# A two-layer block on one core: decay, beta and norm rows of the recurrent layer spread by DMA instead of by products

## The reference, cut to what matters

```python
proj = x @ w_in
qkv, z, b_logit, a_logit = split(proj)
qkv = silu(causal_depthwise_conv(qkv, conv_w))          # 4 taps
q = l2_normalize(q) * (Dh ** -0.5)                      # t * rsqrt(sum(t*t) + 1e-6), per head and token
k = l2_normalize(k)
beta = sigmoid(b_logit)
g = cumsum(-exp(a_log) * softplus(a_logit + dt_bias))   # per head, within a chunk
decay = exp(where(causal, g[:, None] - g[None, :], -inf))
a = (k * beta) @ k.T * decay                            # strictly lower part
m = where(strict, a, 0) + I
u, w = solve(m, [v * beta, k * beta * exp(g)])
qk = q @ k.T * decay
k_dec = k * exp(g[-1] - g)
# then: v_new = u - w @ state;  o = (q*exp(g)) @ state + qk @ v_new;  o * rms * silu(z)
```

## Time and profile before

| | us |
|---|---|
| median of three runs | 1905.39 |
| lowest, highest | 1904.49, 1906.96 |
| the profiled execution's own time (its span, first to last instruction) | 1904.5 |
| TensorE busy | 1755.1 (92%) |
| VectorE busy | 748.0 (39%) |
| ScalarE busy | 451.2 (24%) |
| chain that ended last: PE, DMA, DVE, ACT | 75%, 18%, 3%, 2% |

### The profile page before, as it was taken

One profiled execution on the slowest core, in us unless ns is written; L12 is line 12 of the kernel. 1 busy time (PEld: TensorE's weight loads), 2 busy tenths in 40 slices (PEclk: granted clock), 3 DMA queues, 4 the chain that ended last, 5 costly groups with the idle time before them and its releaser, 6 DMA issues.

```text
span 1904.5 us, 23817 instructions
## 1 busy us (share of the span) xinstructions
PE 1755.1 (92%) x9756; PEld 1111.8 (58%) x9756; DVE 748.0 (39%) x1141; ACT 451.2 (24%) x692; POOL 13.3 (1%) x20
## 2 busy tenths in 40 slices
PE   8999999999999999999999898888898888987986
PEld 5799889798479988966543334333343333423332
DVE  3655567675265553154323231222222222213236
ACT  1544456212054441134211101001010000101103
POOL 0000000000000000000000000000000000000000
PEclk9999999999999999899899899999999999988998
DMA  9544441200544443122899999999999999999993
GB/s 395 217 199 189 195 158 68 87 2 1 221 194 198 194 192 140 49 84 72 340 400 428 427 427 426 429 428 424 428 429 428 428 428 428 428 428 427 427 427 160
DMA packets 41329, 545.22 MB, mean 286 GB/s; under 512 B 4736, under 2 KB 4864, under 8 KB 8608
## 3 DMA queue, kind: packets, MB, share of 16 engines
q1 hardware_dynamic: 39088, 536.22, 67.4%
q0 software_dynamic: 1872, 6.82, 1.0%
q10 hardware_dynamic: 288, 1.05, 0.1%
HBM read 540.92 MB, written 3.15 MB: 286 GB/s over the span
## 4 chain that ended last, share of the span: by engine, by line
PE 75%; DMA 18%; DVE 3%; ACT 2%; issue 1%; SPq 0%; DVEq 0%; ACTq 0%
DMA ring<-experts_dram 18%; PE ps L536 6%; PE ps L2190 5%; PE ps L2167 5%; PE ps L2251 4%; PE ps L2212 4%; PE ps L651 3%; PE ps L650 3%; PE ps L649 3%; PE ps L725 3%; PE ps L723 3%; PE ps L724 3%; PE ps L1219 3%; PE ps L1437 2%; PE ps L2304 2%; PE ps L2238 2%
## 5 line engine op out<-in xcount | busy, mean ns | idle before, releaser
L778 DVE TENSOR_TENSOR ring_split<-ring,ring_split 128x1024 fp32r<-128x1024 f32 x156 | 187.2, 1223 | 128.8 <-ACT ring_split L830 128.8
L2190 PE MATMUL ps<-ring,arena 128*32 128x512 f32 x1152 | 159.5, 704 | 83.2 <-DMA ring<-experts_dram 83.1
L2684 DVE TENSOR_SCALAR arena<-ps 128x512 f32<-128x512 f32 (+1 forms) x38 | 21.5, 565 | 495.6 <-PE ps L2190 202.7
L830 ACT CAST ring_split<-ring 128x1024 fp32r<-128x1024 f32 x156 | 160.4, 1047 | 166.6 <-PE ps L725 92.0
L2212 PE MATMUL ps<-ring,arena 128*128 128x512 f32 x384 | 167.4, 594 | 0.2 <-DMA ring<-experts_dram 0.2
L2990 ACT ACTIVATE arena<-arena 128x512 f32<-128x512 f32 (+1 forms) x38 | 20.1, 530 | 575.7 <-DVE arena L2684 575.7
L2190 PEld LDWEIGHTS ps<-ring,arena 128*32 128x32 f32 x1152 | 41.5, 127 | 190.3 <-issue 184.5
L723 PE MATMUL ps<-arena_split,ring_split 128*128 128x256 f32 x512 | 145.4, 284 | 0.0
L725 PE MATMUL ps<-arena_split,ring_split 128*128 128x256 f32 x512 | 145.0, 283 | 0.0
L724 PE MATMUL ps<-arena_split,ring_split 128*128 128x256 f32 x512 | 144.5, 282 | 0.0
L2212 PEld LDWEIGHTS ps<-ring,arena 128*128 128x128 f32 x384 | 73.1, 191 | 88.4 <-issue 86.4
(11 more groups left out here) (438 smaller groups left out, 2532.6 us busy)
## 6 DMA issues: line engine op xcount, KB each, us to landing
ring<-experts_dram SPq DMA_DIRECT2D x192, 2048.0 KB, 20.0
ring<-weights_dram SPq DMA_DIRECT2D x55, 2048.0 KB, 11.6
row_buf<-rows_dram POOLq DMA_DIRECT2D x13, 512.0 KB, 10.0
ring<-weights_dram SPq DMA_DIRECT2D x3, 1024.0 KB, 11.0
tab<-tables_dram SPq DMA_DIRECT2D x1, 2160.5 KB, 31.8
tab<-weights_dram SPq DMA_DIRECT2D x1, 1536.0 KB, 25.7
gate_mid<-weights_dram SPq DMA_DIRECT2D x1, 1536.0 KB, 28.0
x<-tokens_dram SPq DMA_DIRECT2D x1, 1024.0 KB, 4.9
```

Source lines behind the costliest of these rows:

```text
L778: V.tensor_tensor(low, raw, high, ALU.subtract).then_inc(sem("part_low"), 1)
L830: A.copy(split_buffer(MLP_SPLIT_SLOT, buffer)[0], raw).then_inc(sem("part_high"), 1)
L2190: ins = T.matmul(view(bank(0)[TINY * q:TINY * q + TINY], (2, 256)), xs_of(4 * c + d, j)[:, 0:TINY], w[q // 2][:, d, :, 256 * (q % 2):256 * ...
```

## The change

The four kinds of rows are no longer spread by products. SyncE writes the gate and beta rows (8 partitions) to a new tensor in device memory, `heads_rows` of 4 rows of 2048 values, and reads each row back to all 128 partitions by a broadcast load of 1 MB into ring slots whose weights have been used: the gate to TI, beta to LT, the k norms to TT, the q norms to PR. VectorE then reads SBUF where it read PSUM. The norm sums go to four column tiles of 32 (partitions 0, 32, 64, 96, two heads each), in the order k, q, and directly behind the first z chunk; the square root and the reciprocal work on all 128 partitions. ScalarE takes over KD, KBG and VB, as 32 copies of 128x128 with a scale per partition. TensorE turns k ahead of the products k by k. The clearing of `g_small` by GpSimd and the waits for it go.

```diff
-        rowsT, root8 = rowsT_all[0:8], root_all[0:8]
+        rowsT, root = view(g_small[0:8, 256:768], (2, TILES, P)), view(g_small[:, 768:1280], (2, SEQ))
+        spread_beta, spread_gate, spread_k, spread_q = LT, TI, TT, PR
...
-            def heads_out(rows_, half_, done):
-                pick = table("pick_head")
-                for h in range(4 * half_, 4 * half_ + 4):
-                    m = T.matmul(pair01[:, h * SEQ:(h + 1) * SEQ], pick[:, h * P:(h + 1) * P], rows_, start=True, stop=True,
-                                 skip_group_check=True)
-                m.then_inc(sem(done), 1)
-
+            def square_sums():
+                head_col = table("head_col")
+                pe.wait_ge(sem("gdn_conv"), 5)
+                pe.wait_ge(sem("gdn_sq"), 2)
+                for n, src in ((1, k_squares), (0, pre)):
+                    for row_ in range(2):
+                        for j in range(4):
+                            m = T.matmul(ps[32 * j:32 * j + 32, 0, 512 * n:512 * n + SEQ],
+                                         head_col[:, HEADS * row_:HEADS * row_ + 32], src[:, row_, j * SEQ:(j + 1) * SEQ],
+                                         start=row_ == 0, stop=row_ == 1, skip_group_check=True)
+                    m.then_inc(sem("gdn_sum_psum"), 1)
+
+            z(0, 0)
+            square_sums()
+            for c in range(1, 4):
+                z(0, c)
             for c in range(4):
-                z(0, c)
+                z(1, c)
...
+        def sp_gdn_rows_out(sp):
+            sp.wait_ge(sem("gdn_rows"), 2)
+            sp.dma_start(heads_rows[0:2].rearrange("n (h c) -> h n c", h=HEADS), rowsT.rearrange("p n t c -> p n (t c)"))\
+              .then_inc(sem("gdn_rows_kept"), 16)
+        def sp_gdn_spread(sp, n, to, done="gdn_spread"):
+            sp.dma_start(to, heads_rows[n:n + 1, :].to_broadcast((P, HEADS * SEQ))).then_inc(sem(done), 16)
+        def sp_gdn_rows_in(sp):
+            sp.wait_ge(sem("gdn_rows_kept"), 16)
+            sp.wait_ge(sem("part_low"), gdn_chunk(4, 3) + 1)
+            sp_gdn_spread(sp, 0, spread_gate)
+            sp_gdn_spread(sp, 1, spread_beta)
+        def sp_gdn_norms(sp):
+            for i, n in enumerate((1, 0)):
+                sp.wait_ge(sem("gdn_rnorm"), i + 1)
+                for row_ in range(2):
+                    to = heads_rows[2 + n, 4 * SEQ * row_:4 * SEQ * (row_ + 1)].rearrange("(j c) -> j c", j=4)
+                    sp.dma_start(to, root[row_:row_ + 97:32, n, :]).then_inc(sem("gdn_rows_kept"), 16)
+            sp.wait_ge(sem("part_low"), gdn_chunk(5, 3) + 1)
+            sp.wait_ge(sem("gdn_rows_kept"), 16 + 4 * 16)
+            sp_gdn_spread(sp, 3, spread_k, "gdn_k_spread")
+            sp_gdn_spread(sp, 2, spread_q, "gdn_rows_kept")
...
             for n in range(6):
                 taps(n)
-                highs(n + 2, range(3))
+                highs(n + 2, range(1 if n == 5 else 3))
+                if n == 5:
+                    roots()
+                    highs(n + 2, range(1, 3))
...
             A.activation(z_silu, ps[:, 2:4, :], ACT.Silu).then_inc(flag_up("gdn_z"), 1)
+            a.wait_ge(*flag("gdn_bg"))
+            a.wait_ge(sem("gdn_exp"), 2)
+            a.wait_ge(*flag("gdn_k_psum"))
+            for h in range(HEADS):
+                A.activation(KD[:, h * P:(h + 1) * P], system(pair01, h, 0), ACT.Copy, scale=system(DEC, h, 0)[:, P - 1:P])
+                m = A.activation(KBG[:, h * P:(h + 1) * P], system(pair01, h, 1), ACT.Copy, scale=bg[:, h, 1:2])
+            m.then_inc(flag_up("gdn_k_ready"), 1)
+            a.wait_ge(*flag("gdn_v_psum"))
+            for h in range(HEADS):
+                for t in range(TILES):
+                    m = A.activation(system(VB, h, t), system(pair23, h, t), ACT.Copy, scale=beta[:, h, t:t + 1])
+            m.then_inc(flag_up("gdn_v_ready"), 1)
...
-                lows(n + 2)
+                lows(n + 2, range(1 if n == 5 else 4))
+            for i, n in enumerate((1, 0)):
+                v.wait_ge(sem("gdn_root"), i + 1)
+                V.reciprocal(root[:, n, :], root[:, n, :]).then_inc(sem("gdn_rnorm"), 1)
+            lows(GDN_UNITS - 1, range(1, 4))
...
         def pe_gdn_scores(pe):
+            pe.wait_ge(sem("gdn_conv"), 6)
+            pe.wait_ge(sem("gdn_root"), 2)
+            pe.wait_ge(sem("gdn_unit"), 2)
+            for h in range(HEADS):
+                for t in range(TILES):
+                    m = T.transpose(system(pair01, h, t), qkvT[:, 8 + h, t * P:(t + 1) * P], ident)
+            m.then_inc(flag_up("gdn_k_psum"), 1)
             pe.wait_ge(*flag("gdn_z"))
...
+            v.wait_ge(sem("gdn_spread"), 32)
...
+            v.wait_ge(sem("gdn_qkv"), 6)
+            v.wait_ge(sem("gdn_k_spread"), 16)
+            unit_(1, 1, spread_k)
+            unit_(1, 0, spread_k)
...
+            v.wait_ge(sem("gdn_rows_kept"), 16 + 5 * 16)
+            unit_(0, 1, spread_q)
+            unit_(0, 0, spread_q)
...
-            v.wait_ge(*flag("gdn_k_psum"))
-            V.tensor_tensor(g3(KD), heads16(pair01)[:, :, 0, :], last_col, ALU.mult)
-            V.tensor_tensor(g3(KBG), heads16(pair01)[:, :, 1, :], bg[:, :, 1:2].to_broadcast((P, HEADS, P)), ALU.mult)
...
-            v.wait_ge(*flag("gdn_v_psum"))
-            V.tensor_tensor(g3(VB), g3(pair23), spread(beta.rearrange("p h t -> p (h t)"), P), ALU.mult)
...
             for n in range(5, GDN_UNITS):
+                if n == GDN_UNITS - 1:
+                    sp_gdn_rows_out(sp)
                 fill(sp, f"gdn_in{n}", n % 4, "part_low", gdn_chunk(n - 3, 0))
+            sp_gdn_rows_in(sp)
+            sp_gdn_norms(sp)
             fill(sp, "gdn_out0", 4, "part_used", gdn_chunk(GDN_UNITS, 0))
```

More of the change, by code:

```diff
@@ L257, in lay_out, with build @@
     return {k: np.ascontiguousarray(v) for k, v in arrays.items()}, places
-def build(nc, places, tokens, weights, experts, rows, expert_b, b_down, ple_in, small, tables, bands, parts, out):
+def build(nc, places, tokens, weights, experts, rows, expert_b, b_down, ple_in, small, tables, bands, parts, heads_rows, out):
     with ExitStack() as ctx:
@@ L1155, in pe_gdn_scores @@
             pe.wait_ge(sem("gdn_unit"), 4)
-            for h in range(HEADS):
-                for t in range(TILES):
-                    m = T.transpose(system(pair01, h, t), qkvT[:, 8 + h, t * P:(t + 1) * P], ident)
-            m.then_inc(flag_up("gdn_k_psum"), 1)
             pe.wait_ge(*flag("gdn_LT1"))
```

85 lines of the change are left out of this document (20 added, 65 removed).

## The result

The changed kernel takes 1890.96 us (median of 4 runs, 1888.31 to 1892.21); the kernel before takes 1905.04 beside it (4 runs, 1904.49 to 1906.96). The ratio is 0.9922 [0.9908, 0.9936]: faster by 14.1 us, where 16.6 were forecast. The time lies inside the forecast's own range, 1886.5 to 1891.5. Two executions of the kernel before, timed beside after_again, took 2522 and 6166 us and count nowhere in this document.

The account below looks back on a forecast made before the run. TensorE's issue was taken to bound 341 to 373 us, the experts' weight stream the end. Profiled 1904.5 - 16.3 (k by q earlier) - 0.3 (VB) + 0.9 gave 1888.8 us; range 1886.5 to 1896.5, own case to 1891.5.

Parts of the forecast that it names:

- the forecast's own range: Whole kernel, if the forecast's own case holds: 1886.5 to 1891.5 us around 1888.8; chance 0.60.
- The bound and the removed work: TensorE's issue sets 341 to 373 us; spreads' 14.0 us go, norm sums fall from 7.00 to 2.7.
- The DMA path: Norm rows written in 2.1 us, spread in 5.2: k lands at 351.1, VectorE waits 0.4 us.
- Up to LT: First half of k by k is done, and LT can start, at 358.7; VectorE is free at 358.4.
- LT to k by q: LT and MT of both halves take 3.66 us as before; k by q starts at 362.3, -16.3 us.
- the rival of 0.10: Clock falls behind TensorE's waits around turned k, k by k, k by q: 2.7 us more, 1891.5; chance 0.10.
- VB on ScalarE: Ahead of level 1 of the inverse: 16 copies take 4.2 us, level 1 goes on 0.3 us earlier.
- Passing on: Behind the layer, the whole gain reaches the experts' stream; rival that it does not: 1905, chance 0.03.

Follow-up runs that it names:

- after_again: The changed kernel unchanged, timed again beside the kernel before: 1892.99 us, ratio 0.9929.
- pool_late: The changed kernel with GpSimd's product of silu(z) and norm_w waiting until both masked copies MT are made: 1889.03 us, ratio 0.9912; again on another chip 1893.98 us.
- pool_in_pieces: The changed kernel with GpSimd's product of z as 16 instructions of 128x128 in place of one of 128x2048: 1893.02 us, ratio 0.9922.
- copies_on_vector: The changed kernel with KD, KBG and VB as three VectorE products, as before the change: 1894.18 us, ratio 0.9945.
- norms_later: The changed kernel with two more spreads of the q norms, each waited for, ahead of the k norms' spread: 1900.12 us, ratio 0.9972.
- masks_behind: GpSimd's z product put off, z activation in halves, both LT ahead of both MT, second half of k turned behind k by k: 1890.78 us, ratio 0.9914.
- k_turned_behind: pool_late with turned k placed behind k by k again: 1888.33 us, ratio 0.9908.
- after: The changed kernel itself, against the kernel before: 1890.96 us, ratio 0.9922.

## Why the prediction was right

**The bound and the removed work: right.** TensorE's issue set the stretch, and the z products end 24.6 us behind the first. The forecast, counted from the same first product (329.51 in the order of time of before), has 354.8 - 329.5 = 25.3. The sums took 1.86 us, near the lower bound of 1.8; I took 2.7 from rows of 30-column products. The forecast said that this is worth 0.3 us at most, since VectorE sets the end then. VectorE did not: it was done with the q norms at 356.05, 27.4 us behind the first z product (forecast 358.4, that is 28.9), and then waited 1.32 us for k by k.

**The DMA path: right, with room.** SyncE and the landing:

```profile
340.02 2.61 SPq L1034 DMA_DIRECT2D heads_dram<-arena  x4
343.78 0.80 SPq L1019 DMA_DIRECT2D ring<-heads_dram  x2
```

```profile
ring<-heads_dram SPq DMA_DIRECT2D x4, 1024.0 KB, 4.8
```

The last write is issued by 342.63 and the spreads at 343.78, so writing took under 1.2 us (2.1 taken); a spread lands in 4.8 (5.2 taken). k lands near 348.5, and VectorE takes it up at 349.15 without a wait.
By the Trainium skill's 6.15 us for 1 MB ("DMA: Bandwidth & Descriptors", "Measured (HBM→SBUF, 128 partitions, SWDGE, issued from GpSimd)") k would have landed, as an estimate, 1.35 us later. The trace, with 4.8 us, does not agree for these loads, which SyncE issues.

**Up to LT: right.** LT starts 28.77 us behind the first z product; the forecast's 358.7 is 29.19 (358.7 - 329.51). The 0.42 us are what the shorter sums leave at LT.

**LT to k by q: wrong by 1.75 us.** The step was "LT and MT of both halves to the start of k by q take what they took, 3.66 us". They took 5.41 (357.38 to 362.79). GpSimd's product of silu(z) had moved with the z activation onto the first MT. I followed what the flag of z releases on TensorE and not what it releases on GpSimd. pool_late and pool_in_pieces show this cause: with GpSimd put off the same step takes 3.76 us (358.71 to 362.47).
The Trainium skill had the rule, in "SBUF — State Buffer", section "SBUF: two separate sides": GpSimd and a VectorE operation with two SBUF inputs exclude each other for a whole instruction. The traces agree: MT reads two SBUF tiles and ends 1.08 us behind GpSimd's end, while LT, which reads PSUM, takes its 1.22 beside it.

**The clock: the rival of 0.10 came in part.** k by q took 5.45 us instead of 3.85, 1.6 us more (2.7 in the rival's sum). The step "idleness is expected short: 0.2 us for the z activation and 1 to 2 for LT" failed: TensorE waited 3.73 us, longer by GpSimd's 1.66. But pool_late had the wait of about 2 us that the forecast counted on, and the clock fell in both of its executions, so the step that failed is that such a wait is short enough. What the runs show of waits ahead of k by q and its duration at once behind:

| wait | k by q |
|---|---|
| 0.24, 0.53, 1.41 | 3.84, 3.81, 3.81 |
| 2.08, 2.08, 2.17 | 5.44, 5.40, 5.44 |
| 3.73, 3.76, 3.69 | 5.44, 6.32, 6.31 |
| 5.36 | 6.59 |
| 3.75 (copies_on_vector), 2.08 (norms_later) | 3.81, 3.81 |

Up to 1.41 us no wait in this table was followed by the low level of 1.2 GHz, nor were those of 1.72 us ahead of the P products; the wait of 1.99 ahead of P in masks_behind was, and most longer ones. Three were not: the two of the last row, and the 2.06 us ahead of k by k in k_turned_behind. A place that none of the experiments touches says the same. In every trace TensorE waits 2.07 or 2.08 us ahead of the L976 product that starts between 293.4 and 295.1, the one whose wait the prediction's rival rests on. In the 3 us behind it the clock is 0.50 to 0.62 in ten traces and 1.00 in three: after, copies_on_vector and k_turned_behind. In after:

```profile
294.02 0.36 PE L976 MATMUL ps<-arena_split,ring_split 128*128 128x256 f32 x1 [2.08 <-DVE ring_split L778]
```

```profile
294.02:297.02 3.00, 3.00 (x25) 3.00 (x26) 3.00 (x3) 0.00 (x0) 0.00 (x0) 1.00 0.00 0
```

So a wait of some 2 us can bring the low level and need not, with the same program; the difference between two executions of one kernel here is chance in time as far as these runs go, and what decides is open. copies_on_vector has TensorE's list of after in the same order. One window of both, after first (PE busy, ..., the clock third from the end):

```profile
364.00:367.00 3.00, 3.00 (x17) 3.00 (x16) 0.00 (x0) 0.00 (x0) 0.00 (x0) 0.50 0.25 104
```

```profile
364.00:367.00 3.00, 3.00 (x30) 3.00 (x29) 2.53 (x3) 0.00 (x0) 0.00 (x0) 1.00 0.27 115
```

Both are busy throughout; one issues 17 rows at 0.50 of the full clock, the other 30 at 1.00.

The rule of the Trainium skill that transposes do not count as busy in the same way ("TensorE: Matmul & The Clock Gate", "Part 4: PE-mode transpose") would make turned k and turned v nearly idle time. Turned v, 1.91 us, and the wait of 1.72 behind it run in after without a fall at the next products, which take their 2.05 (clock 1.00 from 370 to 376), and so in the other kernels (waits of 1.12 to 1.73) but masks_behind, where the wait is 1.99; and in k_turned_behind turned k and 0.24 of wait were followed by a full clock. The runs do not show the rule here.

**VB on ScalarE: right.** 0.3 us; the copies follow each other in 4.24 us for 16 (forecast 4.2).

**Passing on: right.** See the table: 501.34 and 500.99 us from level 1 to the first expert load.

The sum by its steps, in us of the start of level 1: -0.4 up to LT, +1.75 for MT, +1.6 for the clock, on a forecast of -16.6, makes -13.65; measured -13.65. The medians say -14.1. The mechanism was right but for these two steps; that the time still lies inside the forecast's own range is in part luck, since the same kernel took 1892.99 in after_again. The experts' part, 3.2 us shorter in this one profiled execution of after than in that of before, varies by 6 us from execution to execution without a pattern by kernel, and nothing is claimed from it.

## What to carry to other kernels

When a change moves a completion earlier, list everything it releases on every engine, and lay each against what the neighbours do at the new time; a GpSimd operation between SBUF tiles does not go beside a VectorE operation with two SBUF inputs. Expect TensorE's products behind a wait of about 2 us to run at either level of the clock, and price both: in this study that is 1.6 us on k by q. Turned k moved into such a wait went with a level 1 that started 1.6 us earlier (49.12 to 47.55), by the clock, in one profiled execution; whether the move kept the clock up is not shown. With executions of one kernel up to 11 us apart (1887.70 to 1899.13 for copies_on_vector), judge a change of 1 us by the distance between two named instructions of the trace.

## What was not expected of the hardware

A VectorE instruction of 1.22 us with two SBUF inputs took 2.88 and 4.28 beside one GpSimd instruction, and 1.32 to 1.47 beside the same work in pieces. GpSimd loses as well: 5.19 and 6.82 us instead of 4.52, the latter with two VectorE products of together 2.35 us beside its start. A row read from device memory to 128 partitions, 1 MB, landed in 4.8 us (median of four; the slowest in 6.9). Products of 32 columns with 256 to stream took 0.058 and 0.059 us a row, whether or not neighbours went to the same columns of the array. The same wait of 2.08 us at the same place of the same program was followed by the full clock in one execution of the changed kernel and by the low one in another (294.02 in after, 294.91 in after_again).
